# Gate stage of a two-layer encoder: five U blocks as plain fp32 products between the gate batches, activations copied by DMA, first query computed by halves

## The reference

```python
def _peer(h, w_query, sub_keys, expert_u, expert_v):
    q = (h @ w_query).reshape(bsz, seq, PEER_HEADS, PEER_QUERY_DIM)
    s1 = einsum('bshk,hnk->bshn', q[..., :half], sub_keys[0])
    s2 = einsum('bshk,hnk->bshn', q[..., half:], sub_keys[1])
    t1, i1 = top_k(s1, 16); t2, i2 = top_k(s2, 16)
    cand = (t1[..., :, None] + t2[..., None, :])
    top_s, top_c = top_k(cand, 16)
    experts = e1 * 128 + e2            # e1, e2: picked out of i1, i2 by top_c
    gates = softmax(top_s)
    act = gelu(einsum('td,ted->te', h_c, expert_u[e_c]))
    out = einsum('te,ted->td', g_c * act, expert_v[e_c])
```

## Time and profile before

| | us |
|---|---|
| median of 3 runs (2115.74 to 2118.91) | 2116.72 |
| the profiled execution, its own time | 2114.93 |
| its span in the profile | 2113.1 |
| first batch to end of the last, layer 1 | 402.56 to 494.36 |
| PE busy | 2013.9 (95%) |
| DVE busy | 1594.4 (75%) |
| ACT busy | 1025.4 (49%) |
| POOL busy | 694.4 (33%) |

### The profile page before, as it was taken

The page is one execution under the profiler, slowest core; times in us unless marked ns, Lnnn a source line. Parts: engine busy times, 40 slices in busy tenths (PEclk is TensorE's granted clock), DMA queues, the critical chain, the costliest instruction groups (busy, mean ns, idle before and its releaser), DMA issues.

```text
span 2113.1 us, 37179 instructions
## 1 busy us (share of the span) xinstructions
PE 2013.9 (95%) x11526; PEld 1675.6 (79%) x11526; DVE 1594.4 (75%) x3065; ACT 1025.4 (49%) x1737; POOL 694.4 (33%) x537
## 2 busy tenths in 40 slices
PE   6999999988999999999989999998899999999997
PEld 5764899887887888888867559998878788888886
DVE  6992677787779977777779738778867788777775
ACT  3543454695345444444444425548943544444443
POOL 6992566772000400000059817666700012000000
PEclk9999999999999999999999999999999999999998
DMA  5223554203558555555422235442055665555553
GB/s 193 94 71 125 180 182 160 100 22 123 194 198 292 186 192 189 189 189 189 140 91 100 90 134 194 163 157 71 11 179 193 206 219 180 194 186 193 184 193 110
DMA packets 90973, 330.42 MB, mean 156 GB/s; under 512 B 10452, under 2 KB 14676, under 8 KB 88573
## 3 DMA queue, kind: packets, MB, share of 16 engines
q1 hardware_dynamic: 90860, 329.23, 46.0%
q10 hardware_dynamic: 16, 0.02, 0.0%
HBM read 326.04 MB, written 3.16 MB: 156 GB/s over the span
## 4 chain that ended last, share of the span: by engine, by line
PE 75%; POOL 7%; issue 7%; DVE 5%; DVEq 2%; ACT 2%; DMA 1%; POOLq 1%; ACTq 0%; SPq 0%
PE ps L849 31%; PE ps L812 14%; PE ps L822 12%; PE ps L826 5%; PE ps L859 3%; POOL arena L1805 3%; POOL v_raw L1805 3%; PE ps L776 3%; PE ps L610 2%; DVE arena L1315 2%; POOL u_raw L1805 1%; PE ps L645 1%; PE ps L728 1%; DVE arena L1485 1%; PE ps L605 1%
## 5 line engine op out<-in xcount | busy, mean ns | idle before, releaser
L849 PE MATMUL ps<-v_hl,w_hl 128*128 128x512 f32 x3072 | 731.6, 392 | 14.7 <-DVE v_hl L1315 14.6
L849 PEld LDWEIGHTS ps<-v_hl,w_hl 128*128 128x128 f32 x3072 | 575.8, 189 | 142.1 <-DVE v_hl L1315 20.9
L822 PE MATMUL ps<-h_hl,u_hl 128*128 128x512 f32 x1152 | 418.3, 397 | 0.0
L1805 POOL TENSOR_TENSOR arena<-arena 128x256 f32<-128x256 f32 (+1 forms) x225 | 213.8, 983 | 371.3 <-DVE arena L1315 368.3
L1315 DVE TENSOR_TENSOR v_hl<-v_raw,v_hl 128x1024 fp32r<-128x1024 f32 x208 | 258.5, 1243 | 45.9 <-ACT v_hl L1141 42.0
L826 PE MATMUL ps<-h_hl,u_hl 128*128 128x256 f32 x1008 | 282.6, 280 | 0.0
L1141 ACT ACTIVATE v_hl<-v_raw 128x1024 fp32r<-128x1024 f32 x208 | 218.9, 1053 | 112.1 <-PE ps L849 96.6
L1315 DVE TENSOR_TENSOR u_hl<-u_raw,u_hl 128x1024 fp32r<-128x1024 f32 x148 | 187.0, 1263 | 114.2 <-ACT u_hl L1103 113.3
L822 PEld LDWEIGHTS ps<-h_hl,u_hl 128*128 128x128 f32 x1152 | 216.4, 188 | 45.1
L1103 ACT ACTIVATE u_hl<-u_raw 128x1024 fp32r<-128x1024 f32 x144 | 152.4, 1058 | 135.0 <-PE ps L822 134.7
L1250 ACT ACTIVATE act_w<-act_w 128x256 f32<-128x256 f32 x144 | 60.1, 417 | 301.5 <-DVE act_w L1750 301.5
(11 more groups left out here) (181 smaller groups left out, 2895.7 us busy)
## 6 DMA issues: line engine op xcount, KB each, us to landing
u_raw<-in_expert_u SPq DMA_DIRECT2D x208, 512.0 KB, 3.3
v_raw<-in_expert_v SPq DMA_DIRECT2D x208, 512.0 KB, 3.3
v_raw<-in_expert_u SPq DMA_DIRECT2D x48, 512.0 KB, 4.2
u_raw<-in_expert_v SPq DMA_DIRECT2D x48, 512.0 KB, 3.3
arena<-in_w_in SPq DMA_DIRECT2D x16, 512.0 KB, 3.8
arena<-in_w_in SPq DMA_DIRECT2D x8, 1024.0 KB, 5.1
arena<-in_ssm_b SPq DMA_DIRECT2D x16, 512.0 KB, 4.3
arena<-in_w_out SPq DMA_DIRECT2D x4, 2048.0 KB, 9.5
```

The costliest lines, as they stand in the source:

```text
L822: return pe.matmul(both, hl[:, 0, k, :], h_hl[:, :, k, :], start=(k == 0), stop=(k == DC - 1))
L849: m = pe.matmul(ps[:, 2 * a + half, :], w_hl[s][:, wp, a * P:(a + 1) * P], v_hl[s][:, vp, half * 512:(half + 1) * 512], start=(first and j ...
L1805: return pool.tensor_tensor(o, a, b, op)
```

## The change

- **Raw products.** Blocks 51 to 55 (`RAW` = 5) are no longer split. PE multiplies `u_raw` by an unsplit copy of `hT` as fp32, 8 products of 256 columns for a block, and each of the 40 products stands by itself after a gate batch: after four of five batches, from batch 0 on. The splits of these five blocks go away on ACT, DVE and POOL, and the counts of `s_u_lo` and `s_u_hi` become `SPLIT` = 123 per layer.
- **The copy.** `hT` lies under the later gates, so it is copied by one DMA of 1 MB, SBUF to SBUF, into `h_raw`, which is the buffer `v_hl[1]`. SP issues it between the loads of blocks 49 and 50, after a wait for the end of all 48 early ups (`s_u_mm`). The loads of blocks 53 to 55 wait for the product that frees their buffer. ACT waits for the copy at batch 0.
- **First query.** The query of head 0 is computed for tokens 0 to 127 before the second transposes and for 128 to 255 behind them, into bank 1; two of four `keep_busy` products go. The query weights of heads 0 and 1 go into buffers that are free earlier (`attn_f`, `slots`, `v_sb`), and are loaded after `s_mixn` instead of behind the spill of `x`. ACT copies this query and its scores before it waits for the spill.

```diff
-GAP_AHEAD = 10
+RAW = AHEAD - FREE_AHEAD
+SPLIT = PK - RAW
...
+        h_raw = v_hl[1][:, :, :].rearrange("p r n -> p (r n)").bitcast(F32).rearrange("p (k t) -> p k t", k=DC)
...
+                for s in range(2):
+                    sp.wait_ge(s_mixn, 4 * l + 2 * s + 2)
+                    load_head(s, s)
+
+                sp.wait_ge(s_x1, TT * (l + 1))
+                sp.dma_start(x_d.ap(), xs_f).then_inc(s_spill, 16)
...
-                for c in range(EARLY, EARLY + AHEAD):
-                    sp.wait_ge(s_u_lo, l * PK + c - (3 if c < EARLY + 2 else 1))
+                for c in range(EARLY, EARLY + FREE_AHEAD + 2):
+                    sp.wait_ge(s_u_lo, l * SPLIT + c - (3 if c < EARLY + 2 else 1))
                     load_u(l, c, c % 2)
+                    if c == EARLY + 1:
+                        sp.wait_ge(s_u_mm, 2 + l * PK + EARLY)
+                        sp.dma_start(h_raw, hT).then_inc(s_hraw, 16)
+                for c in range(EARLY + FREE_AHEAD + 2, EARLY + AHEAD):
+                    sp.wait_ge(s_u_mm, 2 + l * PK + c - 1)
+                    load_u(l, c, c % 2)
...
-                keep_busy(4, 3)
+
+                def first_query(a):
+
+                    pe.wait_ge(s_hT, (2 * l + 1) * 4 + 2 * a + 2)
+                    pe.wait_ge(s_wq[0], 32 * (l * (PH // 2) + 1))
+                    for k in range(DC):
+                        m = pe.matmul(ps[:, 1, a * P:(a + 1) * P], wq_slot[0][:, k, :], hT[:, k, a * P:(a + 1) * P],
+                                      start=(k == 0), stop=(k == DC - 1))
+                    if a:
+                        m.then_inc(s_q, 1)
+
+                first_query(0)
+                keep_busy(2, 3)
                 pe.wait_ge(s_xn, 4 * l + 4)
                 transposes(xn, 1, s_tr)
...
+                def raw_chunk(n):
+
+                    j, k = divmod(n, DC)
+                    j += FREE_AHEAD
+                    if k == 0:
+                        pe.wait_ge(s_u_ld[j % 2], 16 * (l * U_LD + EARLY_LD + j // 2 + 1))
+                        if j == FREE_AHEAD:
+                            pe.wait_ge(s_hraw, 16 * (l + 1))
+                        if j == 4:
+                            pe.wait_ge(s_gelu, 2 + l * PK + EARLY)
+                    o = AHEAD_HALF[j] * S
+                    m = pe.matmul(ps[:, AHEAD_BANK[j], o:o + S], u_raw[j % 2][:, k, :], h_raw[:, k, :],
+                                  start=(k == 0), stop=(k == DC - 1))
+                    if k == DC - 1:
+                        m.then_inc(s_u_mm, 1)
...
-                pe.wait_ge(s_hT, (2 * l + 2) * 4)
-                query(0, 0, 0)
+                first_query(1)
...
-                    if t % GAP_AHEAD == GAP_AHEAD - 3 and ahead < AHEAD:
-
-                        if ahead == 4:
-                            pe.wait_ge(s_gelu, 2 + l * PK + EARLY)
-                        up_ahead(EARLY + ahead, ahead, early_hl[ahead % 4])
-                        ahead += 1
-                assert ahead == AHEAD
-
-
+                    if t % 5 < 4 and chunk < RAW * DC:
+                        raw_chunk(chunk)
+                        chunk += 1
+                assert chunk == RAW * DC
...
-                high_ahead(3)
...
-                    if t in split:
-                        high_ahead(split[t])
+                    if t == 0:
+                        act.wait_ge(s_hraw, 16 * (l + 1))
...
-                    if t in low_after:
-                        low_ahead(low_after[t])
...
-                for j in range(4):
+                for j in range(FREE_AHEAD):
                     low_ahead(l, j)
```

More of the change, by code:

```diff
@@ L185, in encoder @@
         mixn = hT_f.rearrange("p (a n) -> p a n", a=TT)
-        wq_slot = b_f.rearrange("p (s k n) -> p s k n", s=2, k=DC)
+        wq_slot = [f.rearrange("p (k n) -> p k n", k=DC) for f in (attn_f, slots)]
+        key_slot = v_sb
         at[0] = big
         assert big + DC * D + TT * D >= EARLY * S
-        key_slot = take(2 * P).rearrange("p (s n) -> p s n", s=2)
         def again(words):
@@ L333, in encoder @@
         s_u_mm = sem("s_u_mm")
+        s_hraw = sem("s_hraw")
         s_v_mm = sem("s_v_mm")
@@ L479, in head_loads @@
                         c = h * HEAD_UPS + j + 4
-                        sp.wait_ge(s_u_lo, l * PK + c - 3)
+                        sp.wait_ge(s_u_lo, l * SPLIT + c - 3)
                         early_u(c, (s * HEAD_UPS + j) % 4)
-                for s in range(2):
-                    load_head(s, s)
                 with sp.Fori(0, PH // 2 - 1) as hp:
@@ L805, in up @@
                 def up(c, hl, bank, o):
-                    n = l * PK + c
-                    pe.wait_ge(s_u_lo, n + 1)
+                    pe.wait_ge(s_u_lo, l * SPLIT + c + 1)
                     terms = ((0, 0), (0, 1), (1, 0))
@@ L816, in up_wide @@
                 def up_wide(c, hl, bank):
-                    pe.wait_ge(s_u_lo, l * PK + c + 1)
+                    pe.wait_ge(s_u_lo, l * SPLIT + c - RAW + 1)
                     both = ps[:, bank, :].rearrange("p (r t) -> p r t", r=2)
@@ L858, in query @@
                     for k in range(DC):
-                        m = pe.matmul(ps[:, 6, 0:S], wq_slot[:, s, k, :], hT[:, k, :],
+                        m = pe.matmul(ps[:, 6, 0:S], wq_slot[s][:, k, :], hT[:, k, :],
                                       start=(k == 0), stop=(k == DC - 1))
@@ L902, in _ @@
                 pe.wait_ge(s_selT, l + 1)
-                ahead = FREE_AHEAD
+                chunk = 0
                 for t in range(N_BATCH):
@@ L1158, in gelu, with copy_q @@
                     act.activation(act_w[:, j % 2, :], ps[:, AHEAD_BANK[j], o:o + S], ACT.Gelu).then_inc(s_gelu, 1)
-                def copy_q(h):
+                def copy_q(h, bank=6):
                     act.wait_ge(s_q, l * PH + h + 1)
-                    act.activation(qh, ps[:, 6, 0:S], ACT.Copy).then_inc(s_qh, 1)
+                    act.activation(qh, ps[:, bank, 0:S], ACT.Copy).then_inc(s_qh, 1)
                 def copy_scores(h):
@@ L1184, in head @@
                             copy_scores(h + 1)
+                copy_q(0, 1)
+                copy_scores(0)
                 act.wait_ge(s_spill, 16 * (l + 1))
-                copy_q(0)
-                copy_scores(0)
                 high_early(2, 2, 0, False)
@@ L1202, in _ @@
                 act.activation(sel_T[:, 2, :], ps[:, 3, 0:S], ACT.Copy).then_inc(s_selT, 1)
-                split = {1: 4, 5: 5, 13: 6, 23: 7}
                 def hot_squares(t):
@@ L1713, in low_u @@
                 def low_u(c, s):
-                    dve.wait_ge(s_u_hi, l * PK + c + 1)
+                    dve.wait_ge(s_u_hi, l * SPLIT + c - RAW + 1)
                     tt(u_hl[s][:, 1, :, :], u_raw[s][:, :, :], u_hl[s][:, 0, :, :].bitcast(F32), ALU.subtract)\
@@ L1807, in low_early @@
             def low_early(l, c, k):
-                pool.wait_ge(s_u_hi, l * PK + c + 1)
+                pool.wait_ge(s_u_hi, l * SPLIT + c + 1)
                 tt(early_hl[k][:, 1, :, :], early_raw[k].rearrange("p (k n) -> p k n", k=DC),
@@ L1812, in low_ahead @@
             def low_ahead(l, j):
-                pool.wait_ge(s_u_hi, l * PK + EARLY + j + 1)
+                pool.wait_ge(s_u_hi, l * SPLIT + EARLY + j + 1)
                 tt(early_hl[j % 4][:, 1, :, :], u_raw[j % 2][:, :, :],
```

14 lines of the change are left out of this document (3 added, 11 removed).

## The result

| | before | after |
|---|---|---|
| median of 4 runs, same chip (us) | 2116.33 (2115.74 to 2118.91) | 2103.88 (2101.45 to 2106.74) |
| ratio, 95% interval | | 0.9944 (0.993 to 0.9959) |
| profiled execution, own time / span | 2114.93 / 2113.1 | 2101.45 / 2099.6 |

The account below looks back on a forecast made before the run. It took DMA to bound the first query and ACT, in a loop with PE, DVE and POOL, the gate stage. -5.9 + 6.7 - 5.5 = -4.7 us a layer, -9.4 in all, gave 2107 us, range 2097 to 2119.

Parts of the forecast that it names:

- First query: From w_out to the first early up: weights wait removed, half the query ahead of the transposes; -5.9 us a layer.
- The other branch: At the first query, the clock falls all the same: -2.7 us a layer instead of -5.9.
- The fourth load: Ahead of the gate stage, block 50's load stands behind the copy and PE waits 5.5 us; +6.7 us a layer.
- both of my bounds: Landing of block 50's load: 396.1 as if alone, 401.2 if the copy takes twice its time.
- The clock's share: Transposes and block 50's up ahead of the gate stage, slowed by a clock at 0.50: 1.2 us.
- Gate stage: First to last gate batch: five ups and ACT's splits go, 40 products come; -5.5 us a layer, bounds -8.2 and +3.2.
- the floor: Gate stage if ACT never waits: 29 steps of 2.68 us, 77.7 instead of 85.9, a gain of 8.2 us.
- The downs: Behind the gate stage: the downs and the 3.2 us between last batch and first down keep their lengths.
- The copy that does not hold the load up: Rival ahead of the gate stage: block 50 lands near 396.1, clock kept; +2.9 instead of +6.7, 2099.7 us; chance 0.15.
- Both gains small: Rival: clock falls before the first query (-2.7), gate stage gives 3.4; +0.6 a layer, 2118 us; chance 0.18.
- Products in series: Rival in the gate stage: each product delays the next batch by 0.43 us; +4.0 a layer, 2124.7 us; chance 0.10.

Follow-up runs that it names:

- light_act: late_copy with only the first of ACT's four squares computed from the third set on; 2086.02 us, one run.
- light_both: late_copy with the cuts of both five_products and light_act; 2078.64 us, one run.
- five_products: late_copy with 35 of the 40 plain fp32 products left out, only the last of each raw block computed; 2089.71 us, one run.
- load_first: The changed kernel with SP's wait left in place but the load of block 50 issued ahead of the copy; 2098.91 us, ratio 0.9924.
- late_copy: The changed kernel with the copy of the activations issued behind the load of block 51; 2091.08 us, and 2093.1 us when run again.
- filled_stall: The changed kernel with 12 keep_busy products ahead of PE's wait for the selection; 2102.79 us, ratio 0.9951.

## Why the prediction was right

**First query: right.** -5.88 and -6.05 for -5.9. From the end of `w_out`, which is 209.10 by the table's measure, to the first up I had 217.6 - 209.10 = 8.50; it took 8.57. The first half hid in front of the transposes and the DMA wait was gone. The second half took 2.05 us for my 1.75, so that ACT's copy of the query came last (215.24) and not `h_lo` (215.07), for which I had it. The full clock, which I had taken at two to one, held in both layers of this execution but not in all. The other branch was mis-sized: I had priced it at 3.2 us, and it costs 1.43. The second half takes 3.49 then, as I had it (3.5), but the clock is back sooner: the scores take 0.72 for my 1.4, and the first ups run at 1.00.

**The fourth load: right.** This was the term that the diff does not show, and the one that cost most. The load landed 6.98 us after the copy's issue for my 6.3, the chain from ACT's high part to the transposes took 396.54 - 391.81 = 4.73 for my 4.7, the wait 6.01 for 5.5. Where no row of the operation exists, the nearest row of the same kind of traffic (1.5 MB on the same queue) gave 0.7 us too little, and both of my bounds held. The Trainium skill's page "DMA: Bandwidth & Descriptors" (section "Two DMAs through the same engine are not ordered") has descriptors of a queue start in order, but a later one may complete while an earlier one is still writing. No trace here shows the load using that freedom: it landed 1.55 us behind the copy in layer 1 (391.79 and 390.24) and 1.52 in layer 2. The clock's share, 1.04 and 0.73 us, is slightly below my 1.2.

**Gate stage: right in direction and mechanism, the size too small.** The step that failed is the choice inside the bounds. I had worked out three loops of 5.2 to 5.4 us per four batches, argued that loops of one length with few buffers disturb each other, and so put 1.40 us a batch on the first 50. They ran at 66.73/50 = 1.335, half of ACT's 2.68: the floor, all but reached (7.6 and 7.5 of 8.2). The last 14 took 17.47, 1.25 each, for my 1.21. Once under way ACT does not wait, although PE's loop is as long. PE's busy time grew by 1.2 us for my 2.8. The evidence for the floor was in the rows already: ACT's squares at 2.68 apart with no wait noted, late in the stage.

**The downs: nearly.** I had put the gap ahead of the first down at no change; it is 0.28 us longer in both layers. In `light_act` and `light_both` it was back at 3.25, and in `five_products` not, which points to how far behind ACT is at the end of the stage. Which of ACT's instructions it is, was not tried.

**The rivals.** The copy that does not hold the load up fell with `load_first` and `late_copy`. Both gains small: fell too. The clock held at the first query in both layers here and the stage gave 7.6 for its 3.4; the fall that it counted on does occur in other executions, at 1.4 us. Products in series: fell, the stage would have been over 91 us. Against my sum of -4.7 a layer stand -6.0 and -6.6, and the difference is the gate stage's 2.0 to 2.1 less the 0.5 to 0.7 that the wait for block 50 cost more. A further 0.95 of the 13.5 us between the profiled executions lies outside the change. So the middle of the range was missed by two terms that were too small in opposite directions, and not by a wrong mechanism.

## What to carry to other kernels

A wait and a transfer that are put into a DMA queue are paid by the load that stands behind them: read what the next load feeds, and move the new transfer behind the last load that the path needs (here one changed constant took 13.9 us off the two layers, and 8 to 13 off the whole in the two sets of runs, about as much as the whole change). Where an engine's instructions follow each other without a wait at some stretch, look at that pace first for what the stage can fall to; here it fell to it, 40 products on another engine then cost 0.4 us, and relief on one of two nearly equal limits brought 0.4 to 0.6. When run times of one kernel spread by several microseconds, split the span at milestones and compare the granted clock at each pause of TensorE before a cause is named.

## What the runs showed of the hardware

- A copy of 1 MB from SBUF to SBUF and a load of 512 KB behind it took 6.98 us from the first issue to the landing of the load (6.82 in layer 2). Issued ahead of the copy (`load_first`), the load landed 3.92 us after its issue, as long as it took in the kernel before. SP took 0.55 us to issue the copy, 0.33 to issue a load and 0.58 for one right behind the copy.
- A PE that had been idle for 6.01 us ran at a granted clock of 0.50 (1.2 GHz) and was back at 1.00 between 400 and 402, some 4 to 5 us after it started to work. The Trainium skill ("TensorE: Matmul & The Clock Gate", section "What's actually happening") calls the throttled state the default, which activity releases; the rows agree, and twelve products that nobody reads kept the clock at 1.00 (`filled_stall`).
- At shorter pauses the same kernel, `late_copy`, kept the clock in one execution and lost it in another: before the first query (1.43 us a time) and in the mixer (a group of 3.72 us took 5.41). At the first downs it always fell where no products filled the gap, for 6 to 12 products of 0.24 us in 10 us.
- DVE's additions of 128x512 took 0.68 us, or 2.7 to 2.9 where they lay beside a split on POOL for 2.2 us or more. In three layers of 26 this came ten to twelve times instead of two to six: DVE's busy time in 174 us of early ups was 158 to 160 us instead of 133 to 140, and in two of the three PE waited 1.2 us for it (the third, of `load_first`, waited for block 50 anyway).
- An fp32 product of 256 columns takes 0.43 us beside gate batches, and 35 of the 40 cost 0.44 us in the stage (`five_products`), since PE had that room beside ACT.
